# The first attention opens with the value rows of one token tile

## The chip, the core and the metric

The kernel runs on one core of a Trainium2 chip. TensorE (PE) multiplies, VectorE (DVE), ScalarE (ACT) and GpSimd (POOL) work on SBUF and PSUM, SyncE (SP) issues transfers; each of them works through its own queue of instructions in order and waits on semaphores. The metric is the time of one execution in device microseconds.

## The reference

Ten stages on a sequence of 256 tokens of width 1024, in float32. The first is a neighborhood attention; the others (a gated convolution, differential attention, a recurrent mixer and more) are not touched.

```
h   = rms_norm(x, g[0])
qkv = (h @ w_qkv).reshape(B, rows, 64, 3, 16 heads, 64)       # w_qkv: 1024 x 3072
s   = einsum(q / 8, k in a window of 8 x 16 neighbours) + bias
o   = softmax(s) @ v
m   = o @ w_o;  x = x + rms_norm(m, g[1])
```

## The kernel before

**Products.** A float32 matrix is split in two parts of type float32r, high and low (`w_hi`, `w_lo`; `hT_hi`, `hT_lo`), and a product is three matmuls: high x high, high x low, low x high. The tokens are two tiles of 128 (t = 0, 1). `hT` holds the normalised x turned, in 8 blocks of 128 rows, which are made in the order `BLOCKS = [0, 4, 1, 5, 2, 6, 3, 7]`.

**Slabs.** Weights come as slabs of 1 MB in the order of the list that `plan` makes. SP issues them into 3 buffers `raw` (a buffer is free when the slab three earlier is split: `lo_done`), ACT copies a slab into one of 5 buffers `w_hi` (`feed` in ACT's program, L719), DVE subtracts and writes `w_lo` (`feed` in DVE's program, L1298). Each engine calls `feed(n)` at places written out by hand; it works all slabs below n that are not done yet, and waits for each in turn. The first attention has 12 slabs: a column slab holds 256 columns of the query or key weights over all 1024 rows (in DRAM rows of 1 KB), a value slab 512 columns over 512 rows (rows of 2 KB). `COLUMN_SLABS` and `VALUE_SLABS` give their places: before, slabs 0 and 1 are query and key columns, 2 and 3 the first half of the values.

**Opening.** SP issues x's two tiles, slabs 0 to 2, six gain rows, 16 bias rows (`load_rpb`), four rows of taps, and then slab 3. ACT makes the squares of both tiles of x (L735), POOL the reciprocal roots (`powers`) and the high part of slab 0 (L610), DVE scales x (`normed`, L1337), PE turns it (`turn_x`, L2053), ACT and DVE split the turned blocks (`tile_parts`, L738 and L1320), tile 0 and then tile 1. `keep_busy(n)` puts n products of the identity, whose result nobody reads, into PE's queue.

**First attention.** Heads go in pairs (units). PE's order is `first_columns` (banks c0, c1 from slab 0, which starts with tile 1's first block ready), columns c2, c3 (keys, slab 1), scores of units 0 and 1 (`unit_scores`), the taps, then the value rows `value_rows(0, 0, kh, t)` of half 0 from slabs 2 and 3, with unit 0's turn of weights before the last of them. Columns are `half_columns` (24 matmuls of 256 columns of tokens a bank), value rows have 512 columns and one token tile. A result lies in one of 4 PSUM banks in the order of `BANK_ORDER` and is moved out by ACT: `columns_out`, `values_out`, `weights_turned` (L864, L924). Scores wait for the moved q and k. DVE adds the bias (`scores`), takes maxima, ACT the exponentials (`unit_exps`), DVE the quotient (`normalised`). Ahead of this DVE makes lambdas and rotary angles, ACT their sine and an exponential (L1255, L1257).

Of the kernel before, what the change touches and what calls it, by code (L numbers as in the profile page):

```python
# [20 lines left out]
ALU = mybir.AluOpType  # L21
ACT = mybir.ActivationFunctionType
# [18 lines left out]
RAW = 3  # L41
RING = 5
# [26 lines left out]
COLUMN_SLABS = {0: [0, 1, 4, 5, 8, 9, 10, 11], 3: [2, 3, 4, 5, 8, 9, 10, 11]}  # L69
VALUE_SLABS = {0: [2, 6], 3: [0, 6]}  # L70
BANK_ORDER = {0: "c0 c1 c2 c3 taps v0.0 v0.1 T0 c4 T1 c5 V0 V1 c6 c7 v1.0 v1.1 T2 T3 c8 c9 V2 V3 c10 c11 c12 c13"
# [201 lines left out]
def two_blocks(nc, w, out):  # L273
# [3 lines left out]
    with ctx:  # L277
# [82 lines left out]
        invf, ang, rot, turns = z(4096, 4128), z(4128, 4256, (2, T, 32)), z(4256, 4384), z(4384, 4512)  # L360
# [6 lines left out]

        landed = [sem(f"landed{i}") for i in range(RAW)]
        hi_done, lo_done = sem("hi_done"), sem("lo_done")
# [75 lines left out]
        def score_bank(u):  # L445
            return 2 * (u % 2)

# [88 lines left out]
        def _(sp):  # L536
            for t in range(T):
# [3 lines left out]
                    .then_inc(x_loaded[t], 16)  # L541
            for n, (src, k, c, _) in enumerate(slabs):
                if n == RAW:
                    early_rows(sp)
                    load_rpb(sp, 0, rpb_loaded)
                    tap_rows(sp)
# [16 lines left out]
        def _(pool):  # L563
# [43 lines left out]
            late_rows(pool)  # L607
            powers("pre0.1")
            pool.wait_ge(landed[0], 16)
            pool.tensor_copy(w_hi[:, 0, :], raw[:, 0, :]).then_inc(hi_done, 1)  # L610
# [3 lines left out]
            pool.wait_ge(hi_done, 2)  # L614
# [94 lines left out]
        def _(act):  # L709
            fed = [0]  # L710

            def feed(upto):
                while fed[0] < min(upto, n_slabs):
                    n = fed[0]
                    act.wait_ge(landed[n % RAW], 16 * (n // RAW + 1))
# [6 lines left out]
            def feed_half(i):  # L722
# [3 lines left out]
                act.wait_ge(landed[n % RAW], 16 * (n // RAW + 1))  # L726
# [201 lines left out]
            def attention0():  # L928
                b = B[0]
                columns_out(0, 2)  # L930
                columns_out(0, 3)
                feed(b + 4)
                unit_exps(0, 0)
                feed(b + 5)
                unit_exps(0, 1)
                weights_turned(0, 0)
                values_out(0, 0, 0)
                values_out(0, 0, 1)
                feed(b + 7)
                columns_out(0, 4)  # L940
                weights_turned(0, 1)
                feed(b + 8)
                columns_out(0, 5)
                turned_output(0)
                turned_output(1)
                feed(b + 9)
                columns_out(0, 6)
                columns_out(0, 7)
# [289 lines left out]
            for t in range(T):  # L1238
                pre(0, t)
# [1476 lines left out]
```

## Time and profile before

| | |
|---|---|
| median of 3 runs | 1209.8 us (1209.3 to 1210.08) |
| span of the profiled execution | 1208.0 us |
| PE busy | 1189.8 us, 98% |
| DVE, ACT, POOL busy | 939.8, 667.1, 150.4 us |
| mean granted clock of PE | 0.997 |

The span runs from the first to the last instruction of one profiled execution; the time of a run is the whole execution, and the profiled execution has no other time of its own than its span. Busy shares are means over ten stages: an engine that is idle off the chain that ends last costs nothing.

### The profile page before, as it was taken

The numbers are of one execution on the slowest core, as the hardware profiler recorded it, in microseconds if no ns is written. First come the engines' busy times: TensorE is split into PE (matmuls) and PEld (weight loads), VectorE is DVE, ScalarE is ACT, GpSimd is POOL, SyncE is SP. The second block draws the span as 40 slices with busy tenths as digits, with TensorE's granted clock in tenths as the row PEclk, the third lists the DMA queues.
The fourth block names the chain that finished last, engine by engine and source line by source line (L and its number), as shares of the span: only waits on it lengthen the run. The fifth ranks groups of instructions, "written<-read, shape, count | busy, mean of one in ns | idle before, by whom it ended". The sixth has DMA issues, their size and how long they took to land.

```text
span 1208.0 us, 17902 instructions
## 1 busy us (share of the span) xinstructions
PE 1189.8 (98%) x6979; PEld 1038.1 (86%) x6979; DVE 939.8 (78%) x1270; ACT 667.1 (55%) x1060; POOL 150.4 (12%) x275
## 2 busy tenths in 40 slices
PE   8999999999999999999999999999999999999997
PEld 7898888888889988888888988888897888888886
DVE  6767898888776679989887889777775968667765
ACT  5665654444767776544447755434676555444445
POOL 5300510000200012000002100000208420000002
PEclk9999999999999999999999999999999999999999
DMA  7847386555544445665555565655455146565540
GB/s 245 254 154 232 137 269 209 177 196 170 187 151 150 132 149 200 209 206 178 193 170 185 183 230 182 201 178 170 147 175 174 36 156 211 183 209 184 200 140 36
DMA packets 151640, 215.84 MB, mean 179 GB/s; under 512 B 6970, under 2 KB 116924, under 8 KB 151556
## 3 DMA queue, kind: packets, MB, share of 16 engines
q1 hardware_dynamic: 148092, 207.46, 52.2%
q0 software_dynamic: 1760, 3.94, 1.2%
q10 hardware_dynamic: 1704, 3.28, 0.8%
q8 instruction: 56, 0.92, 0.3%
q14 instruction: 28, 0.23, 0.1%
HBM read 213.60 MB, written 1.06 MB: 178 GB/s over the span
## 4 chain that ended last, share of the span: by engine, by line
PE 91%; DVE 4%; ACT 2%; issue 1%; POOL 1%; DMA 0%; POOLq 0%; ACTq 0%; DVEq 0%
PE work L2408 24%; PE work L2411 13%; PE acc L1996 10%; PE acc L1997 9%; PE acc L1998 9%; PE work L1996 5%; PE work L1998 5%; PE work L1997 5%; DVE w_lo L1298 1%; PE work L2397 1%; PE work L2385 1%; PE work L2399 1%; PE work L2018 1%; PE work L2526 1%; PE acc L2053 1%
## 5 line engine op out<-in xcount | busy, mean ns | idle before, releaser
L1298 DVE TENSOR_TENSOR w_lo<-raw,w_hi 128x2048 fp32r<-128x2048 f32 (+1 forms) x194 | 440.7, 2278 | 60.6 <-ACT w_hi L719 60.6
L719 ACT ACTIVATE w_hi<-raw 128x2048 fp32r<-128x2048 f32 (+2 forms) x193 | 365.2, 1898 | 69.5 <-PE work L2411 60.1
L2408 PE MATMUL work<-hT_both,w_hi 128*128 128x512 f32 x1280 | 318.8, 391 | 0.0
L2408 PEld LDWEIGHTS work<-hT_both,w_hi 128*128 128x128 f32 x1280 | 234.8, 188 | 45.2
L2411 PEld LDWEIGHTS work<-hT_both,w_lo 128*128 128x128 f32 x1280 | 174.6, 190 | 12.5
L2411 PE MATMUL work<-hT_both,w_lo 128*128 128x256 f32 x1280 | 178.5, 282 | 0.0
L1996 PE MATMUL acc<-w_hi,aux_hi 128*128 128x512 f32 x400 | 157.8, 395 | 0.0
L1997 PE MATMUL acc<-w_lo,aux_hi 128*128 128x512 f32 x400 | 156.7, 392 | 0.0
L1998 PE MATMUL acc<-w_hi,aux_lo 128*128 128x512 f32 x400 | 155.8, 390 | 0.0
L1085 ACT ACTIVATE aux_hi<-Z 128x256 fp32r<-128x256 f32 x88 | 36.9, 419 | 195.8 <-DVE Z L1722 107.8
L1693 DVE TENSOR_REDUCE Z<-work 128x256 f32<-128x512 f32 x88 | 60.6, 689 | 90.2 <-PE work L2411 88.5
L1998 PEld LDWEIGHTS acc<-w_hi,aux_lo 128*128 128x128 f32 x400 | 75.1, 188 | 16.5
L1996 PEld LDWEIGHTS acc<-w_hi,aux_hi 128*128 128x128 f32 x400 | 75.4, 189 | 13.7
L1997 PEld LDWEIGHTS acc<-w_lo,aux_hi 128*128 128x128 f32 x400 | 75.5, 189 | 12.2
L591 POOL TENSOR_SCALAR ms<-ssq 128x1 f32<-128x1 f32 x26 | 18.8, 724 | 529.6 <-ACT xn L735 444.6
L1996 PE MATMUL work<-hT_both,w_hi 128*128 128x256 f32 x272 | 78.2, 287 | 0.0
L1997 PE MATMUL work<-hT_both,w_hi 128*128 128x256 f32 x272 | 76.9, 283 | 0.0
L1998 PE MATMUL work<-hT_both,w_lo 128*128 128x256 f32 x272 | 76.9, 283 | 0.0
L864 ACT ACTIVATE Z<-work 128x512 f32<-128x512 f32 (+1 forms) x84 | 41.5, 509 | 52.0 <-PE work L1998 35.2
L1996 PE MATMUL acc<-w_hi,hT_both 128*128 128x512 f32 (+1 forms) x184 | 67.8, 368 | 0.6 <-DVE hT_both L1320 0.6
L1998 PE MATMUL acc<-w_hi,hT_both 128*128 128x512 f32 (+1 forms) x184 | 66.6, 362 | 0.0
L1997 PE MATMUL acc<-w_lo,hT_both 128*128 128x512 f32 (+1 forms) x184 | 66.5, 362 | 0.0
(271 smaller groups left out, 1782.4 us busy)
## 6 DMA issues: line engine op xcount, KB each, us to landing
raw<-in_ffn_w_in SPq DMA_DIRECT2D x44, 1024.0 KB, 5.2
raw<-in_ffn_w_out SPq DMA_DIRECT2D x22, 1024.0 KB, 5.0
raw<-in_w_gate SPq DMA_DIRECT2D x22, 1024.0 KB, 5.3
raw<-in_w_up SPq DMA_DIRECT2D x22, 1024.0 KB, 5.3
raw<-in_w_down SPq DMA_DIRECT2D x22, 1024.0 KB, 5.0
raw<-in_na_w_qkv SPq DMA_DIRECT2D x12, 1024.0 KB, 7.5
raw<-in_da_w_qkv SPq DMA_DIRECT2D x12, 1024.0 KB, 5.3
raw<-in_ple_w_gate SPq DMA_DIRECT2D x8, 1024.0 KB, 5.0
```

Of the source, the lines that this page charges most:

```text
L591: link(pool.tensor_scalar(ms[:, c + p:c + p + 1], ssq[:, c + p:c + p + 1], so_far, None, ALU.add))
L719: act.activation(w_hi[:, n % RING, 0:size], raw[:, n % RAW, 0:size], ACT.Copy).then_inc(hi_done, 1)
L864: act.activation(dst, src, func).then_inc(bank_free[g % WORK], 1)
L1085: act.activation(aux_hi[:, c % 2, :], hid32[:, c % 2, :], ACT.Copy).then_inc(hid_hi_done, 1)
L1298: dve.tensor_tensor(w_lo[:, n % RING, 0:size], raw[:, n % RAW, 0:size], w_hi[:, n % RING, 0:size].bitcast(F32), ALU.subtract).then_inc(lo_ ...
L1693: dve.tensor_reduce(src, bank(g).rearrange("p (e s) -> p s e", e=2), AX.X, ALU.add)\
L1996: pe.matmul(dst, stationary[0], moving[0], start=first, stop=False)
L1997: pe.matmul(dst, stationary[0], moving[1], start=False, stop=False)
L1998: return pe.matmul(dst, stationary[1], moving[0], start=False, stop=last)
L2018: ins = pe.transpose(b[0:width, i * P:i * P + rows], v, ident[0:rows, 0:rows])
L2408: pe.matmul(b.rearrange("p (e s) -> p e s", e=2), v[0][:, k, cols(c % 2)], hT_both[:, k, :, :], start=k == 0, stop=False)
L2411: ins = pe.matmul(b[:, 0:S], v[1][:, k, cols(c % 2)], hT_hi[:, k, :], start=False, stop=k == KT - 1)
```

## The change

Slabs 0 and 1 are now the first half of the values (`VALUE_SLABS` 0 and 6), and columns begin with slab 2. They come in four halves of 0.5 MB, each with two blocks of rows in the order of `BLOCKS`: half 0 between the tiles of x, half 1 behind tile 1, then 2 and 3. ACT makes the high part of halves 0 and 3, POOL of 1 and 2, DVE all four low parts, between its blocks of tile 0. PE begins with `first_rows` of tile 0 (it takes each block as it is split), turns x's tile 1 inside it, does tile 1's rows, then c0 to c3 and the rest. Two calls of `keep_busy` (8 and 2) go. ACT's four loads of lambda, positions, table and gains move behind tile 0's splits. ACT and DVE call `feed` and the evacuations in a new order. The angles lie in another place of `Z`.

```diff
+FIRST = 2
...
-COLUMN_SLABS = {0: [0, 1, 4, 5, 8, 9, 10, 11], 3: [2, 3, 4, 5, 8, 9, 10, 11]}
-VALUE_SLABS = {0: [2, 6], 3: [0, 6]}
-BANK_ORDER = {0: "c0 c1 c2 c3 taps v0.0 v0.1 T0 c4 T1 c5 V0 V1 c6 c7 v1.0 v1.1 T2 T3 c8 c9 V2 V3 c10 c11 c12 c13"
+COLUMN_SLABS = {0: [2, 3, 4, 5, 8, 9, 10, 11], 3: [2, 3, 4, 5, 8, 9, 10, 11]}
+VALUE_SLABS = {0: [0, 6], 3: [0, 6]}
+BANK_ORDER = {0: "v0.0 v0.1 c0 c1 c2 c3 taps c4 c5 T0 c6 T1 c7 V0 V1 v1.0 v1.1 T2 T3 c8 c9 V2 V3 c10 c11 c12 c13"
...
+        half_landed = [sem(f"half_landed{i}") for i in range(2 * FIRST)]
+        act_half_hi, pool_half_hi, half_lo = sem("act_half_hi"), sem("pool_half_hi"), sem("half_lo")
...
+        def landing(n):
+            return 16 * (n // RAW + (n % RAW >= FIRST))
+
+        def weight_half(v, i):
+            return v[:, i // 2, (i % 2) * (SLAB // 2):(i % 2 + 1) * (SLAB // 2)]
...
+            def value_half(i):
+                src = w["na_w_qkv"][0][:, 2 * D:2 * D + 512].rearrange("(b a p) n -> p a b n", b=2, p=P)
+                sp.dma_start(weight_half(raw, i).rearrange("p (b n) -> p b n", b=2), src[:, i, :, :])\
+                    .then_inc(half_landed[i], 16)
...
             for t in range(T):
                 src = w["x"][0]
                 sp.dma_start(x[:, t, :],
                              bass.AP(src.tensor, src.offset + 32 * t * D, [[D, 32], [64 * D, 4], [1, D]]))\
                     .then_inc(x_loaded[t], 16)
+                value_half(t)
+            value_half(2)
+            value_half(3)
             for n, (src, k, c, _) in enumerate(slabs):
+                if n < FIRST:
+                    continue
...
+            powers("pre0.0")
+            for i in (1, 2):
+                pool.wait_ge(half_landed[i], 16)
+                pool.tensor_copy(weight_half(w_hi, i), weight_half(raw, i)).then_inc(pool_half_hi, 1)
             powers("pre0.1")
-            pool.wait_ge(landed[0], 16)
-            pool.tensor_copy(w_hi[:, 0, :], raw[:, 0, :]).then_inc(hi_done, 1)
             for i in range(32):
                 ins = pool.memset(invf[:, i:i + 1], float(np.float32(10000.0) ** np.float32(-i / 32)))
             ins.then_inc(freq_ready, 1)
-            pool.wait_ge(hi_done, 2)
+            pool.wait_ge(hi_done, 1)
...
-                    act.wait_ge(landed[n % RAW], 16 * (n // RAW + 1))
+                    act.wait_ge(landed[n % RAW], landing(n))
...
+                feed(b + 6)
                 columns_out(0, 2)
+                feed(b + 7)
                 columns_out(0, 3)
-                feed(b + 4)
                 unit_exps(0, 0)
-                feed(b + 5)
                 unit_exps(0, 1)
+                feed(b + 8)
+                columns_out(0, 4)
+                columns_out(0, 5)
                 weights_turned(0, 0)
-                values_out(0, 0, 0)
-                values_out(0, 0, 1)
-                feed(b + 7)
-                columns_out(0, 4)
+                feed(b + 9)
+                columns_out(0, 6)
                 weights_turned(0, 1)
-                feed(b + 8)
-                columns_out(0, 5)
+                columns_out(0, 7)
                 turned_output(0)
                 turned_output(1)
...
-                feed(b + 9)
-                columns_out(0, 6)
-                columns_out(0, 7)
...
-            for t in range(T):
-                pre(0, t)
+            def high_half(i):
+                act.wait_ge(half_landed[i], 16)
+                act.activation(weight_half(w_hi, i), weight_half(raw, i), ACT.Copy).then_inc(act_half_hi, 1)
+
+            pre(0, 0)
+            high_half(0)
+            pre(0, 1, (0,))
+            evacuated(act, G["vec"])
+            tile_parts(0, 0, range(4))
+            pre(0, 1, (1,))
+            tile_parts(0, 0, range(4, 8))
+            high_half(3)
...
-            evacuated(act, G["vec"])
-            tile_parts(0, 0)
             tile_parts(0, 1)
-            act.wait_ge(hi_done, 1)
-            fed[0] = 1
+            fed[0] = FIRST
             feed(3)
+            values_out(0, 0, 0)
+            feed(4)
+            values_out(0, 0, 1)
             columns_out(0, 0)
+            feed(5)
             columns_out(0, 1)
...
-                    dve.wait_ge(hi_done, n + 1)
+                    dve.wait_ge(hi_done, n + 1 - FIRST)
...
-                feed(b + 3)
+                feed(b + 5)
                 expand(0)
+                expand(1)
+                feed(b + 6)
                 scores(0, 0)
-                expand(1)
+                scores(0, 1)
                 taps_out()
-                scores(0, 1)
-                feed(b + 4)
+                feed(b + 7)
                 normalised(0)
                 expand(2)
-                feed(b + 5)
                 normalised(1)
                 expand(3)
-                feed(b + 6)
-                feed(b + 7)
+                feed(b + 8)
                 turned_output(0)
                 turned_output(1)
-                feed(b + 8)
...
+            def low_half(i):
+                if i in (1, 2):
+                    dve.wait_ge(pool_half_hi, i)
+                else:
+                    dve.wait_ge(act_half_hi, 1 + i // 3)
+                dve.tensor_tensor(weight_half(w_lo, i), weight_half(raw, i), weight_half(w_hi, i).bitcast(F32),
+                                  ALU.subtract).then_inc(lo_done if i % 2 else half_lo, 1)
...
+            low_half(0)
+            tile_parts(0, 0, range(4))
+            low_half(1)
+            tile_parts(0, 0, range(4, 8))
             normed(0, 1)
-            tile_parts(0, 0)
+            low_half(2)
+            low_half(3)
             tile_parts(0, 1)
-            feed(2)
+            fed[0] = FIRST
+            feed(3)
             lambdas()
             rotary()
+            feed(4)
...
-            def first_columns():
...
+            def first_rows(t, kh):
+                g = G[f"v0.0.{t}"]
+                b = open_bank(pe, g) if kh == 0 else work[:, g % WORK, :]
+                for i in range(4):
+                    k, half = BLOCKS[4 * kh + i], 2 * kh + i // 2
+                    if t == 0 and i % 2 == 0:
+                        if half in (1, 2):
+                            pe.wait_ge(pool_half_hi, half)
+                        else:
+                            pe.wait_ge(act_half_hi, 1 + half // 3)
+                    split_done(pe, 0, t, k)
+                    for part in (hT_hi, hT_lo):
+                        pe.matmul(b, part[:, k, cols(t)], w_hi[:, kh, cols(i, 512)],
+                                  start=kh == 0 and i == 0 and part is hT_hi, stop=False)
+                if t == 0 and kh == 1:
+                    turn_x(0, 1)
+                for i in range(4):
+                    if t == 0 and i % 2 == 0:
+                        pe.wait_ge(lo_done if i else half_lo, kh + 1)
+                    ins = pe.matmul(b, hT_hi[:, BLOCKS[4 * kh + i], cols(t)], w_lo[:, kh, cols(i, 512)],
+                                    start=False, stop=kh == 1 and i == 3)
+                if kh == 1:
                     ins.then_inc(bank_full[g % WORK], 1)
+                elif t == 1:
+                    ins.then_inc(used, 1)
...
-                first_columns()
-                half_columns(0, 2)
-                half_columns(0, 3)
+                for t in range(T):
+                    first_rows(t, 0)
+                    first_rows(t, 1)
+                for n in range(4):
+                    half_columns(0, n)
                 unit_scores(0, 0)
                 unit_scores(0, 1)
                 turn_taps()
-                value_rows(0, 0, 0, 0)
-                value_rows(0, 0, 0, 1)
-                value_rows(0, 0, 1, 0)
+                half_columns(0, 4)
+                half_columns(0, 5)
                 unit_turn(0, 0)
-                value_rows(0, 0, 1, 1)
-                half_columns(0, 4)
+                half_columns(0, 6)
                 unit_turn(0, 1)
-                half_columns(0, 5)
+                half_columns(0, 7)
                 unit_values(0, 0)
                 unit_values(0, 1)
-                half_columns(0, 6)
-                half_columns(0, 7)
...
             turn_x(0, 0)
-            keep_busy(8)
             for ph, kind in enumerate(PHASES):
                 if kind in ("na", "da"):
                     if ph == 0:
-                        turn_x(0, 1)
-                        keep_busy(2)
```

## Rows read from the trace of the kernel before

**Rows 1.** The page: the span.

```profile
span 1208.0 us, 17902 instructions
```

**Rows 2.** PE's waits in the execution: us in total, times, longest.

```profile
PE work L2165 <- DVE hT_both L1320: 2.1, 1, 2.1
...
PE work L2018 <- DVE Z L1531: 1.0, 1, 1.0
```

**Rows 3.** PE in order of time, 14 to 43 us: start, us, engine, line.

```profile
14.96 5.87 PE L2165 MATMUL work<-hT_both,w_hi 128*128 128x256 f32 x32 [2.13 <-DVE hT_both L1320]
...
22.59 0.28 PE L1996 MATMUL work<-hT_both,w_hi 128*128 128x256 f32 x1
...
28.44 0.72 PE L2183 MATMUL acc<-Z 64*128 64x128 f32 x8
...
30.44 0.37 PE L2072 MATMUL work<-ident,Z 88*128 88x88 f32 x2
...
31.11 0.50 PE L1996 MATMUL work<-w_hi,hT_both 128*128 128x512 f32 x1
...
39.46 0.60 PE L2018 MATMUL work<-ident,Z 128*128 128x128 f32 x4
...
42.67 0.28 PE L1996 MATMUL work<-hT_both,w_hi 128*128 128x256 f32 x1
```

**Rows 4.** Busy time by engine in a stretch, granted clock, DMA share, GB/s.

```profile
16.00:19.30 3.30, 3.30 (x17) 3.27 (x16) 3.08 (x5) 3.14 (x6) 0.24 (x2) 0.50 0.79 233
```

**Rows 5.** SP's queue in order of time, 0 to 80 us.

```profile
9.57 13.55 SPq L528 DMA_DIRECT2D Z<-in_na_rpb  x16
...
24.91 37.95 SPq L553 DMA_DIRECT2D raw<-in_na_w_qkv  x9
```

**Rows 6.** Issues by line: ns shortest/median/longest, first and last start (L553: slabs 1 and 2).

```profile
L553 SPq DMA_DIRECT2D raw<-in_na_w_qkv x2: 582/1732/2881, 2.8 to 3.4; - x2
...
L508 SPq DMA_DIRECT2D Z<-in_norm_g x5: 279/296/1509, 6.3 to 8.9; - x5
...
L528 SPq DMA_DIRECT2D Z<-in_na_rpb x16: 677/766/1719, 9.6 to 22.3; - x16
L528 POOL DMA_DIRECT2D Z<-in_na_rpb x16: 563/602/774, 42.8 to 51.7; - x16
```

**Rows 7.** The page's DMA issues: KB each, us to landing (column slabs).

```profile
raw<-in_ffn_w_in SPq DMA_DIRECT2D x44, 1024.0 KB, 5.2
```

**Rows 8.** ACT, DVE and POOL in order of time, 6 to 17 us.

```profile
6.20 0.63 ACT L735 ACTIVATE xn<-x 128x512 f32<-128x512 f32 x1
...
7.35 0.88 DVE L1337 TENSOR_SCALAR xn<-x,rstd 128x512 f32<-128x512 f32 x2 [0.98 <-POOL rstd L596]
...
8.65 0.74 ACT L738 ACTIVATE hT_both<-acc,vecT 128x128 fp32r<-128x128 f32 x2 [1.12 <-PE acc L2053]
...
9.16 2.52 DVE L1337 TENSOR_SCALAR xn<-x,rstd 128x512 f32<-128x512 f32 x2 [0.92 <-POOL rstd L596]
...
9.40 2.00 POOL L610 CAST w_hi<-raw 128x2048 fp32r<-128x2048 f32 x1 [0.35 <-DMA raw<-in_na_w_qkv]
...
16.83 0.61 DVE L1320 SCALAR_TENSOR_TENSOR hT_both<-acc,vecT,hT_both 128x128 fp32r<-128x128 f32 x2 [0.18 <-ACT hT_both L738]
```

**Rows 9.** ACT and DVE in order of time, 16 to 42 us.

```profile
16.96 3.70 ACT L719 ACTIVATE w_hi<-raw 128x2048 fp32r<-128x2048 f32 x2
...
17.36 4.49 DVE L1298 TENSOR_TENSOR w_lo<-raw,w_hi 128x2048 fp32r<-128x2048 f32 x2
...
21.83 0.38 ACT L864 ACTIVATE Z<-work 128x256 f32<-128x256 f32 x1 [1.17 <-PE work L2170]
...
23.20 1.28 ACT L1255 ACT_TABLE_LOAD   x1
...
25.76 0.31 ACT L1255 ACTIVATE trig<-Z 128x128 f32<-128x128 f32 x1 [1.28 <-DVE Z L1948]
...
40.72 0.60 ACT L924 ACTIVATE Z<-work 64x512 f32<-64x512 f32 x1
```

More of the change, by code:

```diff
@@ L359, in two_blocks @@
         lamr, lamp = z(11864, 12120, (2, 2, 64)), z(12120, 12248, (2, 64))
-        invf, ang, rot, turns = z(4096, 4128), z(4128, 4256, (2, T, 32)), z(4256, 4384), z(4384, 4512)
+        invf, ang, rot, turns = z(3584, 3616), z(3616, 3744, (2, T, 32)), z(3744, 3872), z(3872, 4000)
         ebr = z(9216, 9728, None, 8)
@@ L725, in feed_half @@
                 half = slice(i * size, (i + 1) * size)
-                act.wait_ge(landed[n % RAW], 16 * (n // RAW + 1))
+                act.wait_ge(landed[n % RAW], landing(n))
                 if n >= RING:
@@ L1304, in feed_half @@
                 half = slices(slabs[n][1] * slabs[n][2] // 2)[i]
-                dve.wait_ge(hi_done, n + 1)
+                dve.wait_ge(hi_done, n + 1 - FIRST)
                 ins = dve.tensor_tensor(w_lo[:, n % RING, half], raw[:, n % RAW, half],
@@ L2154, in half_columns @@
                 ins.then_inc(bank_full[g % WORK], 1)
-            def first_columns():
-                v = w_hi[:, 0, :].rearrange("p (k n) -> p k n", k=KT)
-                pe.wait_ge(hi_done, 1)
-                for c in range(2):
-                    b = open_bank(pe, G[f"c0.{c}"])
-                    for k in BLOCKS:
-                        if c == 0:
-                            split_done(pe, 0, 1, k)
-                        for part in (hT_hi, hT_lo):
-                            pe.matmul(b[:, 0:S], v[:, k, cols(c)], part[:, k, :], start=k == 0 and part is hT_hi, stop=False)
-                v = slab(0)[1]
-                for c in range(2):
-                    g = G[f"c0.{c}"]
-                    for k in range(KT):
-                        ins = pe.matmul(work[:, g % WORK, 0:S], v[:, k, cols(c)], hT_hi[:, k, :],
-                                        start=False, stop=k == KT - 1)
+            def first_rows(t, kh):
[20 more added lines that the diff above has]
+                if kh == 1:
                     ins.then_inc(bank_full[g % WORK], 1)
+                elif t == 1:
+                    ins.then_inc(used, 1)
             def unit_scores(ph, u):
@@ L2376, in first_tile @@
                     for i in range(2):
-                        pe.wait_ge(hi_done, b0 + i + 1)
+                        pe.wait_ge(hi_done, b0 + i + 1 - FIRST)
                     for k in ks:
```

## The prediction

> **What bounds the kernel now.** I read the page first (the span), then who waited for whom on TensorE, then the instructions in order of time in the first 60 us, then SyncE's queue. The span is 1208.0 us [rows 1] and the median of the runs 1209.8, so 1.8 us lie around the span; the sum below is made within the span and carried over to 1209.8. TensorE's longest wait in the whole execution is the one ahead of its first product (2.1 us), and the one hole that it meets later in the first attention is 1.0 us, before a turn of softmax weights [rows 2]. So the kernel is a row of products, and what the opening can win or lose is the time at which that row gets past the first attention's first columns. The reader is to see five points on TensorE [rows 3]: the first product at 14.96, columns c0 and c1 done at 22.59, c2 and c3 at 28.44, scores and taps done at 31.11, the first half of the values done at 42.67. The 48 value products took 11.56 less the 0.35 of the turn that lies among them (39.46 to 39.81): 11.2 us, 0.233 each. Columns c2 and c3 took 5.85 for 48, or 0.122 each, 2.9 a bank. Scores take 1.0 a unit, the taps 0.67.
>
> In the changed order the same work, c0 to c3, both value tiles, two scores and the taps, ends with the taps. Before had all of it at 42.67 - 0.35 = **42.3**. What the change brings is the time at which the new order gets there, less 42.3, because from there on the two orders hold the same products.
>
> **The opening.** The work on x's tile 0 stays: its squares end at 6.20, DVE scales it at 7.35, ACT's first split of a turned block starts at 8.65 [rows 8]. The first half slab takes the queue place of x's tile 1, which was there by 6.20. ACT copies half a slab in 0.95 (half of 1.85), DVE makes a low half in 1.1 (half of 2.25) [rows 9], so the low half runs from 8.25 to 9.35 behind the scaling, the first low block is ready at 9.7, and TensorE starts there: **5.2 us earlier** than 14.96. It doesn't run through. On DVE now lie, one behind the other: four low blocks to 10.9 (0.79 for two [rows 8]), the second low half to 12.0, four blocks to 13.5, tile 1's scaling (0.88) to 14.4, two low halves to 16.7, and tile 1's eight blocks to 19.8. Tile 0's products end inside that, at about 17; tile 1's follow without a hole, 24 x 0.233 = 5.6, to 22.7. The third slab (c0, c1) is copied by ACT after tile 1's splits, from 19.6 to 21.4, and by DVE to 23.7; c0 and c1 then end at 23.7 + 5.8 = 29.5.
>
> The two casts on POOL are the weak place. Now a scaling pair that takes 0.88 alone took 2.52 where POOL's cast of a slab (9.40, 2.00) lay over it [rows 8]. So a cast beside a DVE instruction can cost from 0 up to its own length, 1.0 for a half, twice: c1 ends between 29.5 and 31.5. I take 30.5. The Trainium skill (SBUF — State Buffer, "SBUF: two separate sides") says that a VectorE instruction with two SBUF inputs and a GpSimd instruction that reads SBUF exclude each other for the whole instruction. That speaks against giving POOL two casts beside DVE's low halves; the 2.52 agrees with such an exclusion, and by that rule c1 would end at 31.5.
>
> If nothing else were late, TensorE would now be 3.4 us ahead: at 30.5 it lacks c2, c3, scores and taps, 5.8 + 2.67 = 8.4, and before stands 8.4 ahead of its 42.3 at 33.9; 33.9 - 30.5 = 3.4.
>
> **What is late next: the fourth slab.** Columns c2 and c3 need the slab of key columns, number 3. Before used slab 3 only for the second half of the value rows' sum, at 31.11 + 24 x 0.233 = 36.7. It is the first that SyncE issues behind the bias rows and taps, and it was issued at 24.91, though its buffer was free earlier [rows 5]. The change leaves that order, and puts two more issues ahead of it. How early can it go? In before three issues were held up: the third slab's (2.88 against 0.58), the first gain row's (1.51 against 0.30) and one of the bias rows' (1.72 against 0.68) [rows 6]: 2.3 + 1.2 + 1.0 = 4.5 us. Two more issues cost 1.2. From below, with no hold-up left: 24.9 - 4.5 + 1.2 = 21.6. From above, with all of it kept: 26.1. The halves have rows of 2 KB where slabs 0 and 1 had 1 KB, so fewer packets stand ahead, and the two extra issues pass while the queue drains; I keep one hold-up of the smaller kind, 1.1: **22.7**. The Trainium skill (Perfetto Trace Analysis, "DMA Instruction — HWDGE (DVE, Sync)") has the profiled time of an issue hold the wait for the descriptor generator and the generation, which runs into a full buffer. By that page fewer rows ahead mean shorter issues, which would move the sum to the lower bound; no row of before shows which of the three was which.
>
> From 22.7: a column slab lands 5.2 us after its issue where the queue is empty [rows 7]: 27.9. ACT's copy 1.85: 29.8. DVE's low part 2.3: **32.1**. So c2 starts at 32.1, not at 30.5, and the 1.0 to 2.0 of the casts and any slow clock in the opening are covered by this wait: the cover is 1.6 us on my value, and what goes over it is paid one for one. c3 ends at 37.9.
>
> **And the fifth: ACT's order.** ACT is the engine behind the scores, and its queue is in order. From 29.8 it has: tile 1's value rows, two activations of 0.60 [rows 9], to 31.0; c0, 0.3, 31.3; slab 4, landed 3.2 after slab 3 (the spacing of 6.20 and 9.40 [rows 8]) at 31.1, copied to 33.2; c1 33.5; the sine with its table load, 1.28 + 0.31, 35.1; the exponential's table load 36.4; then feed(b + 6), slab 5, 38.3; and only then c2, 38.7. c2 had been ready in PSUM since 35.0. unit_scores(0, 0) needs it, so it runs from 38.7 to 39.7; feed(b + 7) holds c3 until 40.9; unit_scores(0, 1) from 40.9 to 41.9; taps to **42.6**. Slabs 4 to 6 land in time for this: slab 5's buffer is free at 23.7, slab 6's at 32.1, and it has until 38.7. The table loads and slab copies hid behind products before; here they lie on the path, 1.7 us of it (a path of c3's end at 37.9, 0.35 for its evacuation, 2.67 for scores and taps would give 40.9).
>
> **The sum.** 42.6 - 42.3 = **+0.3 us**: of the 5.2 us won at the first product DVE's queue leaves 3.4; slab 3 takes 1.6 of it, c3's evacuation 0.35, ACT's order 1.7. As a line: end = issue of slab 3 + 19.9. From the bounds 21.6 and 26.1: 41.5 to 46.0, or -0.8 to +3.7.
>
> Behind it I price the rest at nothing. The first turn of weights needs the softmax of unit 0: DVE makes slab 4, two expansions, slab 5, two scores, the taps and slab 6 first and reaches the weights at about 47.4; TensorE has c4 and c5 until 42.6 + 5.8 = 48.4. That cover is 1.0 us; without it the turn would wait the difference. The hole at 108 hangs on the last two units' scores and softmax [rows 2], which move with TensorE, so it neither gives nor takes. The moved ACT issues (lambda, positions, table, gains: four) fall at about 15, where ACT waits for tile 1's turn; the removed ten filler products were no one's input, but they kept TensorE busy: see the clock.
>
> **Rivals.** (1) **The gain is kept**: slab 3 isn't late. It decides from an issue at about 20.0 on. That wants the bias rows to go out at POOL's pitch (0.60 each [rows 6]) instead of SyncE's 13.55 for 16 [rows 5]: 13.55 - 9.6 = 4.0 earlier than 22.7, so 18.7, low part at 28.1. Then the path is c1 at 30.5, c2 and c3, evacuation, scores and taps: 39.4, -2.9: **1206.9**. For it: before held issues up while much traffic stood ahead. Against it: the shortest bias row was 0.68 on SyncE, held up or not. (2) **The queue is held as before**, the slower side: slab 3 goes out at or after 24.9. It decides from there: 24.9 + 19.9 = 44.8, +2.5, **1212.3**, and at 26.1 **1213.5**. For it: the bytes ahead of the fourth slab are the same, and the issue comes two places later. Against it: the biggest hold-up belonged to a third whole slab, and there are fewer rows. (3) **The clock**: in before the granted clock was 0.50 (1.2 of 2.4 GHz) from 16.0 to 19.3 [rows 4], after the stretch in which TensorE waited 2.1 us, and the 32 products there took 5.87 instead of 32 x 0.122 = 3.9: 2.0 lost. The new opening has shorter but more waits and no fillers. A low stretch before c1's end is covered by slab 3; one on c4 to c7, after the waits of the scores, is paid in full: +0.3 + 2.0, **1212.1**; with a somewhat later slab 3 it passes the bound. That the change alters nothing that can be told is the likeliest case itself.
>
> **How the numbers follow.** A measurement of this kernel tells about 0.2% (2.4 us) from no change. The likeliest case, slab 3 issued between 21.6 and 24.8, has 0.52: -0.8 to +2.4, 1209.0 to 1212.2, at 1210.1. Rival 1 has 0.18; rival 2 0.2; rival 3 0.1, half of it within the bound beside an early slab 3. Faster by over 0.2%: 0.2 (rival 1, and 0.02 for a shorter ACT path in the likeliest). Slower by over 0.2%: 0.27 (rival 2, half of rival 3, 0.02 for casts that go over their cover). Within: the remaining 0.53. The range reaches to rival 1's time and near the upper bound of slab 3: 1206.9 to 1213.2.
>
> **What would show it.** Right: TensorE's first product near 9.7; a wait of TensorE's columns for DVE's low part of 1 to 3 us that ends near 32; SyncE's slab 3 near 22.7; waits of the score products for ACT's evacuations near 38 and 41 that follow slab copies; the taps near 42.6; the rest of the trace shifted by the same amount. Wrong: no wait for slab 3 (rival 1), its issue after 24.9 (rival 2), a clock of 0.50 behind the scores (rival 3), or a wait of the first turn of weights for DVE, which I priced at nothing.

## The result

The changed kernel takes 1212.1 us (median of 9 runs, 1210.8 to 1213.4) against 1209.3 for the kernel before beside it (9 runs): a ratio of 1.0027, 95% interval 1.0019 to 1.0035. It is **slower by 2.8 us**, inside the prediction's range. The 0.2% that the prediction takes as no change lies just inside the interval. The likeliest case ended at +2.4 and at 1212.2: the difference is just outside it, the time just inside, because the kernel before measured 1209.3 here and 1209.8 ahead of the prediction. The times of the kernel before lie in two groups some 2 us apart (of the 15 beside experiments 8 to 10, seven from 1207.5 to 1208.2 and eight from 1209.3 to 1210.4), so its median depends on the mix, and its profiled execution (span 1208.0) is of the upper group. The profiled execution of the changed kernel took 1212.35 with a span of 1210.6 and a mean granted clock of 0.996.

Who TensorE waited for in the changed kernel (us in total, times, longest; line 2038 is the column products, 1327 DVE's low part of a slab):

```profile
PE work L2038 <- DVE w_lo L1327: 4.7, 2, 4.2
...
PE work L2060 <- DVE Z L1560: 1.0, 1, 1.0
PE work L2210 <- DVE hT_both L1349: 0.9, 1, 0.9
```

In [rows 2] no slab was waited for; now one costs 4.2 us. In order of time on TensorE, to be held against [rows 3]:

```profile
9.95 2.06 PE L2210 MATMUL work<-w_hi,hT_both 128*128 128x512 f32 x8 [0.91 <-DVE hT_both L1349]
...
24.78 0.39 PE L2038 MATMUL work<-hT_both,w_hi 128*128 128x256 f32 x1 [0.44 <-DVE w_lo L1327]
...
35.03 0.58 PE L2038 MATMUL work<-hT_both,w_hi 128*128 128x256 f32 x1 [4.23 <-DVE w_lo L1327]
...
39.66 0.28 PE L2038 MATMUL work<-hT_both,w_hi 128*128 128x256 f32 x1
...
42.98 0.71 PE L2233 MATMUL acc<-Z 64*128 64x128 f32 x8
43.98 0.72 PE L2233 MATMUL acc<-Z 64*128 64x128 f32 x8
...
45.64 0.38 PE L2038 MATMUL work<-hT_both,w_hi 128*128 128x256 f32 x1
```

The first product comes 5.0 us earlier (14.96 to 9.95). c1 is done at 24.78 + 5.85 = 30.6, where before had the same amount of work done at 33.9: 3.3 ahead. Then TensorE stands until 35.03 (4.23 us of it is the wait for slab 3's low part). Scores and taps are done at 45.64, where before stood at 42.3: +3.3. Later points that both kernels share are late by 2.8 (scores of units 2 and 3 from 59.23, before from 56.40; the ffn's first product at 143.4, before at 140.6; the last product of that line at 1165.0, before at 1162.4, which is 2.6), so next to nothing is won back behind the opening.

SyncE's queue of the changed kernel, against [rows 5]; and the gain rows' issues (ns shortest/median/longest), against [rows 6]:

```profile
4.47 0.53 SPq L572 DMA_DIRECT2D raw<-in_na_w_qkv  x1
5.04 4.93 SPq L517 DMA_DIRECT2D Z<-in_norm_g  x5
...
10.36 12.79 SPq L537 DMA_DIRECT2D Z<-in_na_rpb  x16
...
24.93 31.40 SPq L572 DMA_DIRECT2D raw<-in_na_w_qkv  x8
```

```profile
L517 SPq DMA_DIRECT2D Z<-in_norm_g x5: 295/296/3455, 5.0 to 9.7; - x5
```

Slab 3 goes out at 24.93, before at 24.91. It lands at 30.74, where ACT had waited for it 7.11 us. Behind it come the copies of slabs 4 (34.03), 5 (39.26) and 6 (41.33), with the evacuations of c2 (41.06) and c3 (43.13) among them (ACT, in order of time):

```profile
30.74 1.91 ACT L740 ACTIVATE w_hi<-raw 128x2048 fp32r<-128x2048 f32 x1 [7.11 <-DMA raw<-in_na_w_qkv]
...
34.03 1.91 ACT L740 ACTIVATE w_hi<-raw 128x2048 fp32r<-128x2048 f32 x1
...
39.26 1.90 ACT L740 ACTIVATE w_hi<-raw 128x2048 fp32r<-128x2048 f32 x1
41.06 0.36 ACT L885 ACTIVATE Z<-work 128x256 f32<-128x256 f32 x1
41.33 1.90 ACT L740 ACTIVATE w_hi<-raw 128x2048 fp32r<-128x2048 f32 x1
43.13 0.37 ACT L885 ACTIVATE Z<-work 128x256 f32<-128x256 f32 x1
```

And the stretches behind the wait (columns as in [rows 4]: busy time and count of PE, PEld, DVE, ACT, POOL, then granted clock):

```profile
33.00:36.00 3.00, 0.97 (x4) 0.97 (x5) 2.00 (x2) 2.99 (x5) 0.00 (x0) 0.50 0.89 280
36.00:39.00 3.00, 3.00 (x16) 3.00 (x15) 3.00 (x3) 2.95 (x4) 0.00 (x0) 0.50 0.90 286
39.00:42.00 3.00, 3.00 (x25) 3.00 (x24) 2.26 (x4) 2.99 (x5) 0.00 (x0) 0.90 0.97 307
```

The granted clock is 0.50 (1.2 of 2.4 GHz) where the wait ends. The first 21 column products behind it took 39.66 - 35.03 = 4.63 us; at the 0.122 each of the later ones they are 2.56, so 2.1 are lost.

### The profile page after: what moved, and what is told of

It reads as the page before. It is cut to its first block, busy times and chain, and to the rows that moved or that the text cites. A ratio compares the mean times of both kernels' runs of the same rounds, so it can differ in the third digit from the quotient of the medians.

```text
span 1210.6 us, 17870 instructions
## 1 busy us (share of the span) xinstructions
PE 1188.5 (98%) x6959; PEld 1035.8 (86%) x6959; DVE 939.3 (78%) x1272; ACT 667.4 (55%) x1061; POOL 147.9 (12%) x276
## 4 chain that ended last, share of the span: by engine, by line
PE 90%; DVE 4%; ACT 2%; SPq 2%; issue 1%; DMA 0%; POOL 0%; POOLq 0%; ACTq 0%; DVEq 0%
PE work L2456 24%; PE work L2459 13%; PE acc L2038 10%; PE acc L2039 9%; PE acc L2040 9%; PE work L2038 5%; PE work L2039 5%; PE work L2040 5%; DVE w_lo L1327 2%; PE work L2445 1%; PE work L2433 1%; PE work L2447 1%; PE work L2060 1%; PE work L2574 1%; SPq L537 1%
## 5 line engine op out<-in xcount | busy, mean ns | idle before, releaser
L1327 DVE TENSOR_TENSOR w_lo<-raw,w_hi 128x2048 fp32r<-128x2048 f32 (+1 forms) x192 | 436.0, 2276 | 64.4 <-ACT w_hi L740 64.4
L740 ACT ACTIVATE w_hi<-raw 128x2048 fp32r<-128x2048 f32 (+1 forms) x192 | 363.5, 1898 | 73.0 <-PE work L2459 59.7
L2459 PE MATMUL work<-hT_both,w_lo 128*128 128x256 f32 x1280 | 178.5, 282 | 0.0
L2038 PE MATMUL work<-hT_both,w_hi 128*128 128x256 f32 x288 | 83.9, 291 | 4.7 <-DVE w_lo L1327 4.7
L2039 PE MATMUL work<-hT_both,w_hi 128*128 128x256 f32 x288 | 82.3, 286 | 0.0
L2040 PE MATMUL work<-hT_both,w_lo 128*128 128x256 f32 x288 | 82.2, 286 | 0.0
```

Source lines behind the costliest of these rows:

```text
L740: act.activation(w_hi[:, n % RING, 0:size], raw[:, n % RAW, 0:size], ACT.Copy).then_inc(hi_done, 1)
L1327: dve.tensor_tensor(w_lo[:, n % RING, 0:size], raw[:, n % RAW, 0:size], w_hi[:, n % RING, 0:size].bitcast(F32), ALU.subtract).then_inc(lo_ ...
L2038: pe.matmul(dst, stationary[0], moving[0], start=first, stop=False)
L2039: pe.matmul(dst, stationary[0], moving[1], start=False, stop=False)
L2040: return pe.matmul(dst, stationary[1], moving[0], start=False, stop=last)
L2459: ins = pe.matmul(b[:, 0:S], v[1][:, k, cols(c % 2)], hT_hi[:, k, :], start=False, stop=k == KT - 1)
```

## The experiments

**The theory** after the result: slab 3's place behind the bias rows makes TensorE wait 4.2 us; the low clock comes of the wait; and ACT's order (two slab copies and two table loads ahead of c2 and c3) is a second gate of the scores just behind. **The rivals**: ACT's order alone is the loss; the clock alone is; the hold-up belongs to the gain rows and not to the place in the queue.

Times are medians; the ratio is to the kernel before, run beside each. A trace shows one execution. Fillers are products of the identity whose result nobody reads.

**1. Slab 3 first, nothing else** (slab3_first).

```diff
-                if n == RAW:
+                if n == RAW + 1:
                     early_rows(sp)
                     load_rpb(sp, 0, rpb_loaded)
                     tap_rows(sp)
```

> SyncE issues slab 3 ahead of the gain rows, bias rows and taps; slab 4 comes behind them. Theory S (the late slab 3 is the loss, nothing else): slab 3 goes out near 12.2 us, TensorE's 4.2 us wait ahead of c2 is gone, the taps end at 30.5 + 5.8 + 0.4 + 2.7 = 39.4 instead of 45.6, and the time is 1212.1 - 6.2 = 1205.9. Theory A (ACT's in-order queue is a second gate behind it): slab 4 now lands near 32.5, ACT waits for it with c1's, c2's and c3's evacuations behind, so scores of unit 0 start near 40, of unit 1 near 42.4, taps end near 44.1: 1210.6. Theory C (the low clock on c2 is the loss): the wait and with it the low clock go, 2.2 us: 1209.9.

1217.2 us, ratio 1.0068 (1.0056 to 1.0080): the worst of all. The wait for slab 3 goes (c2 starts at 31.62), but slab 4 is now the one behind the bias rows. ACT meets its copy ahead of c1's, c2's and c3's evacuation. ACT, TensorE and a stretch of this kernel:

```profile
35.88 1.91 ACT L740 ACTIVATE w_hi<-raw 128x2048 fp32r<-128x2048 f32 x1 [7.13 <-DMA raw<-in_na_w_qkv]
...
42.91 0.36 ACT L885 ACTIVATE Z<-work 128x256 f32<-128x256 f32 x1
```

```profile
43.42 1.23 PE L2233 MATMUL acc<-Z 64*128 64x128 f32 x8 [5.78 <-ACT Z L885]
```

```profile
45.00:48.00 3.00, 2.73 (x26) 1.69 (x20) 2.30 (x4) 1.61 (x9) 0.00 (x0) 0.50 0.47 133
```

The wait moved on, grew to 5.78 us, and the low clock came with it (8 score products take 1.23 us instead of 0.71). SyncE's first gain row goes out at 12.84 here, 8 us behind slab 2 and right behind slab 3, and no gain row takes more than 0.52 us: the long issue on the first of them is gone (one bias row takes 1.79).

**2. Bias rows on POOL's queue** (bias_pool).

```diff
-                    load_rpb(sp, 0, rpb_loaded)
...
             ins.then_inc(freq_ready, 1)
+            load_rpb(pool, 0, rpb_loaded)
```

> The 16 bias rows go out on POOL's queue behind its memsets of the frequencies, so slabs 3, 4 and 5 follow their free buffers (about 12, 18, 25 us). Theory S: taps end at 39.4, 1205.9. Theory A: with slab 4 early ACT is held less, scores of unit 0 start near 36.5, unit 1 near 38.4, taps end at 40.1: 1206.6. Theory C: 1209.9. Against all of them: if POOL's 16 issues delay the masks that the bias needs past 38 us, the scores are late on DVE and the first turn of weights waits.

1213.9, ratio 1.0037 (1.0025 to 1.0049). SyncE is free for slab 3 at 12.12. But POOL issues the bias rows from 15.2 to 24.8, and the slab that SyncE issues in that time (18.23) and the one right behind it (24.86) land late:

```profile
L571 SPq DMA_DIRECT2D raw<-in_na_w_qkv x2: 368/378/389, 18.2 to 24.9; - x2
...
DMA to landing us min/median/max: 10.3/12.2/14.1
```

Slab 4 lands 14.1 us after its issue (slab 3 of the changed kernel 5.8), ACT holds c2 behind it, the scores wait 2.97, and the clock is 0.50 to 0.66 from 42 to 51. Taps come 1.3 earlier than in the changed kernel (43.70 against 44.97), the first turn of weights 1.4 later (52.87 against 51.49).

**3. ACT's order alone** (act_order): evacuations ahead of slab copies.

```diff
             values_out(0, 0, 0)
-            feed(4)
             values_out(0, 0, 1)
             columns_out(0, 0)
-            feed(5)
-            columns_out(0, 1)
             act.wait_ge(rot_ready, 1)
...
+            columns_out(0, 1)
+            feed(4)
...
                 feed(b + 6)
                 columns_out(0, 2)
-                feed(b + 7)
                 columns_out(0, 3)
+                feed(b + 7)
```

> ACT moves the value rows, c0 and c1 out and makes the sine and exponential before slab 3 lands, and moves c2 and c3 out before it copies slab 6. Theory A as the prediction had it (ACT's order costs 1.7 us by itself): 1210.4. Theory S, with the clock as it was seen: c3 ends at 43.0 on TensorE anyway, ACT has c2 out at 41.4 and c3 at 43.5, so no more than 0.2 to gain: 1211.9 to 1212.1.

1213.6, ratio 1.0039 (1.0027 to 1.0051): no gain. ACT and TensorE:

```profile
31.72 3.70 ACT L740 ACTIVATE w_hi<-raw 128x2048 fp32r<-128x2048 f32 x2
```

```profile
36.00 0.58 PE L2037 MATMUL work<-hT_both,w_hi 128*128 128x256 f32 x1 [5.13 <-DVE w_lo L1326]
```

TensorE now waits 5.13 us for slab 3, the clock behind it is 0.50, and the scores start at 43.53. The new order has a cost of its own: slab 3 landed at 30.5 (issue at 24.68, 5.8 to landing), but its copy starts at 31.72, behind two table loads and c1's evacuation, so 1.2 us of the wait are ACT's. The run shows that this order gains nothing; it doesn't show what ACT's order costs by itself.

**4. Fillers in the wait** (fill: nine between c1 and c2; fill16: sixteen).

```diff
                 for n in range(4):
+                    if n == 2:
+                        for _ in range(9):
+                            pe.matmul(acc[:, 3, 0:P], ident[:, :], ident[:, :], start=True, stop=True)
                     half_columns(0, n)
```

> Nine products of the identity between c1 and c2 (about 3.9 us of the 4.2 us wait); their result is not read. Theory C (the low clock on c2 is the loss): c2 takes 2.9 us instead of 5.1 and all of it is gained, 1209.9. Theory A: c3 ends near 40.8, but unit 0's scores wait for ACT's c2 at 41.4 and unit 1's for c3 at 43.5, taps at 45.2: 1211.7. Theory S: the wait for slab 3 stays 4.2 us with the fillers in it.

1213.6, ratio 1.0042 (1.0029 to 1.0054). Nine fillers took only 2.2 us (31.0 to 33.1), 2.64 of the wait were left, and the clock was 0.56 from 36 to 39, so this run says nothing on a full clock; the next has sixteen.

> As fill, with 16 products of the identity, 3.9 us, which fill the wait for slab 3 nearly to its end (9 of them had taken 2.2 us and left 2.6 us open, and the clock fell all the same). Theory C: c2 and c3 run at the full clock, 2.2 us less than after's time. Theory A: unit 0's scores then wait for ACT's c2 near 41.4, unit 1's for c3 near 43.5, taps at 45.2 against 45.6: 0.4 us less, and a low clock may come behind those waits instead.

1212.5, ratio 1.0033 (1.0021 to 1.0046). Now the clock is full on c2 and c3 (1.00 from 33 to 45), and what lay behind it shows on TensorE, with a stretch behind the taps:

```profile
35.46 0.39 PE L2038 MATMUL work<-hT_both,w_hi 128*128 128x256 f32 x1 [0.66 <-DVE w_lo L1327]
...
42.01 0.71 PE L2233 MATMUL acc<-Z 64*128 64x128 f32 x8 [0.53 <-ACT Z L885]
44.08 0.71 PE L2233 MATMUL acc<-Z 64*128 64x128 f32 x8 [1.01 <-ACT Z L885]
45.08 0.37 PE L2114 MATMUL work<-ident,Z 88*128 88x88 f32 x2
```

```profile
45.00:48.00 3.00, 3.00 (x23) 2.72 (x16) 2.90 (x10) 2.72 (x15) 0.00 (x0) 0.64 0.95 316
```

The taps start at 45.08, in the changed kernel at 44.97. The 2.1 us of low clock are made up, and a later slab 3 (0.4) and the waits for ACT (1.5) take nearly all of it: the second gate stands at nearly the same point as the first. Behind the waits of 0.53 and 1.01 the clock falls after all, to 0.64 and then 0.79 from 45 to 51, and the first turn of weights comes at 53.09 (changed kernel 51.49). This execution was the slowest of the five (1214.2), so the median may not pay that.

**5. Fillers and ACT's order** (act_fill16): sixteen fillers with experiment 3's order, changed in one place: slab 3's copy (`feed(4)`) and c1's evacuation lie ahead of the exponential, which takes away experiment 3's own delay. The edit is shown against 3.

```diff
+            feed(4)
+            columns_out(0, 1)
             act.wait_ge(lam_sum, 1)
...
-            columns_out(0, 1)
-            feed(4)
...
+                        for _ in range(16):
+                            pe.matmul(acc[:, 3, 0:P], ident[:, :], ident[:, :], start=True, stop=True)
```

> Sixteen fillers, and ACT's order with the exponential's table load behind slab 3's copy and c2 and c3 moved out before slab 6 is copied. If clock and ACT's order hide one another (each alone brings 0 to 0.4 us), both together bring c3's end at 40.8, scores from 41.0, taps at 43.9 against 45.6: 1.8 us less than after, 1 us over before (ratio 1.0009). If only slab 3's lateness counts, no less than after (ratio 1.0027).

1210.5, ratio 1.0017 (1.0008 to 1.0025). Scores at 40.67 and 41.67 without a wait, taps at 42.67. Sixteen fillers alone and experiment 3's order alone gave nothing; fillers and this order bring 1.2 us against the changed kernel by the ratios (1.0027 to 1.0017), with intervals that overlap. What this order brings without fillers was not run.

**6. Fillers in the kernel before** (before_fill): keep_busy(9) in the place of keep_busy(2).

```diff
                         turn_x(0, 1)
-                        keep_busy(2)
+                        keep_busy(9)
```

> The kernel before with seven more products of the identity in TensorE's 2.1 us wait ahead of its first product. Theory C (the low clock follows a wait and costs 2.0 us there): the 32 products take 3.9 us instead of 5.9, time less 2.0 (ratio 0.9983). Rival: the first 16 products are paced by the blocks that DVE splits (0.39 each, the last at 17.4), so full clock brings only 20.7 - 19.6 = 1.1 us (ratio 0.9991). If the clock stays low in spite of the fillers: no change.

1209.0, ratio 1.0001 (0.9992 to 1.0010). In the profiled execution the low stretch of [rows 4] is gone (1.00 from 13 to 19.3, scores at 26.21 instead of 28.44), but the median doesn't move. And most of those 2.2 us aren't the fillers'. DVE, POOL and TensorE:

```profile
9.03 0.88 DVE L1337 TENSOR_SCALAR xn<-x,rstd 128x512 f32<-128x512 f32 x2 [0.92 <-POOL rstd L596]
```

```profile
10.06 1.89 POOL L610 CAST w_hi<-raw 128x2048 fp32r<-128x2048 f32 x1 [1.15 <-DMA raw<-in_na_w_qkv]
```

```profile
13.29 4.85 PE L2165 MATMUL work<-hT_both,w_hi 128*128 128x256 f32 x32
```

In this execution slab 0 landed at 10.06, behind DVE's scaling of tile 1, which took 0.88. In the one of [rows 8] it landed at 9.40, POOL's cast lay over the scaling, and that took 2.52. This is 1.6 us, and the first product came 1.67 earlier here. To the clock at most 1.0 is left: the 32 products take 4.69 (13.29 to 17.98) at 1.00 and took 5.71 (14.96 to 20.67) with the low clock in them. This kernel has two groups of times as well, five from 1207.4 to 1207.8 and six from 1209.0 to 1211.1, and this execution (1207.38) is the lowest of the eleven. That the cast's place makes the two groups fits these two traces, but is not shown.

**7. Slab 3 first and both orders** (reordered): experiment 1, and ACT and DVE work slabs 4 to 7 in other places, so that fewer evacuations and steps of the softmax are queued behind a slab that hasn't landed. ACT's and then DVE's part are shown.

```diff
-                if n == RAW:
+                if n == RAW + 1:
...
-            feed(3)
+            feed(4)
             values_out(0, 0, 0)
-            feed(4)
             values_out(0, 0, 1)
             columns_out(0, 0)
-            feed(5)
             columns_out(0, 1)
...
-                feed(b + 6)
                 columns_out(0, 2)
-                feed(b + 7)
+                feed(b + 5)
                 columns_out(0, 3)
+                feed(b + 6)
                 unit_exps(0, 0)
                 unit_exps(0, 1)
+                feed(b + 7)
...
-            feed(3)
+            feed(4)
             lambdas()
             rotary()
-            feed(4)
...
-                feed(b + 5)
                 expand(0)
                 expand(1)
-                feed(b + 6)
+                feed(b + 5)
                 scores(0, 0)
                 scores(0, 1)
                 taps_out()
-                feed(b + 7)
                 normalised(0)
-                expand(2)
+                feed(b + 6)
                 normalised(1)
+                expand(2)
+                feed(b + 7)
                 expand(3)
```

> Slab 3 is issued ahead of the bias rows, DVE makes its low part right behind slab 2's, ACT moves c2 out before it copies slab 4 and c3 right behind, and DVE makes the bias before slab 4's low part and the weights before slab 5's. Theory S+A (slab 3's place on SyncE and ACT's order together hold the opening's gain back, each alone moves the wait): no wait of TensorE over 1 us up to the taps, no low clock, c2 near 31, c3 done near 36.8, taps done near 40.0 against before's 42.3; with 0.6 lost at slab 5 the time is before less 1.5 to 2.0 us (ratio 0.9984 to 0.9988). Rival M (the queue's bytes are the limit, so the wait moves on again): slab 4, now behind the bias rows, lands near 36, its low part is ready at 40 or later, c4 waits 1 to 3 us and the clock falls behind that wait: before or slower.

1208.1, ratio 0.9997 (0.9988 to 1.0006). No big wait on TensorE and no low clock in the opening:

```profile
36.73 0.72 PE L2231 MATMUL acc<-Z 64*128 64x128 f32 x8
37.73 0.71 PE L2231 MATMUL acc<-Z 64*128 64x128 f32 x8
38.73 0.37 PE L2112 MATMUL work<-ident,Z 88*128 88x88 f32 x2
```

Some 4 us are back against the changed kernel (1.0027 to 0.9997 is 3.6). The 1.5 to 2.0 below the kernel before that were expected aren't there: from before it can't be told. The trace has the taps done at 39.5, earlier than expected, but the 42.3 that they were held against is of an execution of before's upper group; in experiment 6's execution the same point comes at 40.3 (c4 from 40.63, less the 0.35 of the turn).

**8. The two orders without slab 3** (orders_only): experiment 7 with slab 3 in the changed kernel's place.

```diff
-                if n == RAW + 1:
+                if n == RAW:
```

> The reordered kernel's orders of ACT and DVE, but slab 3 back in its place behind the bias rows and taps. Theory (slab 3's issue sets the end, the orders only take away what is queued behind it): issue at 24.9, c2 near 35.0 with a wait of 4 us or more on TensorE, low clock behind it, scores near 42 to 43, taps near 45: 1211 to 1212, 0 to 1 below the changed kernel. Rival (ACT's order was the loss all along): scores near 39 to 40, 1209 or less.

1213.5, ratio 1.0038 (1.0024 to 1.0052). The slab-3 move alone stands at 1.0068, the orders alone at 1.0038, both at 0.9997: neither gains by itself. Expected was 0 to 1 us below the changed kernel, measured 1 above, with overlapping intervals. These orders are made for an early slab 3: ACT copies it ahead of the value rows, so the first value row is moved out at 31.04 (changed kernel 22.43), and with slab 3 late they have a cost of their own. The profiled execution was the fastest of the five (1211.4), and its trace doesn't show what the median pays: slab 3 goes out at 23.89, TensorE waits 2.79 for it, and the clock stays full.

```profile
33.40 0.39 PE L2036 MATMUL work<-hT_both,w_hi 128*128 128x256 f32 x1 [2.79 <-DVE w_lo L1326]
```

**9. Gain rows behind the bias rows** (rows_later).

```diff
-                    early_rows(sp)
                     load_rpb(sp, 0, rpb_loaded)
                     tap_rows(sp)
+                    early_rows(sp)
```

> The changed kernel with the six gain rows issued behind the bias rows and taps instead of ahead of them. Theory (the hold-up belongs to the place in the queue, not to the kind of transfer): the first bias row is held 2 us or more, the gain rows take 0.3 each, slab 3 goes out at 24.5 to 25.5 as before. Rival (the hold-up belongs to the gain rows' own descriptors): the first bias row takes 0.7, slab 3 goes out at about 22 if the gain rows then pass unheld, and TensorE's wait for it shrinks by 2.5.

A single run, 1212.75. SyncE's queue, and the bias rows' issues:

```profile
5.38 15.38 SPq L537 DMA_DIRECT2D Z<-in_na_rpb  x16
...
22.55 1.65 SPq L517 DMA_DIRECT2D Z<-in_norm_g  x5
...
24.58 30.73 SPq L572 DMA_DIRECT2D raw<-in_na_w_qkv  x8
```

```profile
L537 SPq DMA_DIRECT2D Z<-in_na_rpb x16: 677/730/2994, 5.4 to 20.0; - x16
```

The long issue is now the first bias row's, the gain rows take 0.3 each, and slab 3 goes out at nearly the same time (24.58): the hold-up belongs to the place behind the slabs.

**10. Slab 8 behind the second turn** (reordered2): experiment 7 with one more place of ACT changed.

```diff
-                feed(b + 9)
                 columns_out(0, 6)
                 weights_turned(0, 1)
+                feed(b + 9)
                 columns_out(0, 7)
```

> The reordered kernel with one place changed: ACT moves c6 and the second turn of weights out before it waits for slab 8. In the reordered kernel that wait (2.43 us for the slab's landing at 51.17) lay ahead of the turn's evacuation, and TensorE's product of values waited 0.75 us for it. Theory (what is left is ACT's queue in order): that wait goes, the time falls by 0.7 to about 1207.4, 1.4 below before. Rival (the two orders end alike, because scores of units 2 and 3 then wait for c7's evacuation, which now lies behind the copy): the wait shows up at c7, and the time stays at 1208.1.

1207.3, ratio 0.9987 (0.9979 to 0.9996): **faster than before**, by 1.6 us, and than the changed kernel by 4.8 (1.0027 to 0.9987). The wait of the value products for ACT (0.75 in 7) is gone. That this one place brought the gain is not shown: the intervals of 7 and 10 overlap, and the profiled execution (1208.5) is one of the two slowest of eleven, with a wait for ACT and a low clock that the median need not have:

```profile
38.44 0.72 PE L2231 MATMUL acc<-Z 64*128 64x128 f32 x8 [0.71 <-ACT Z L885]
```

```profile
42.00:45.00 3.00, 3.00 (x20) 3.00 (x20) 2.86 (x11) 3.00 (x17) 0.00 (x0) 0.68 0.91 328
```

Nine of the eleven times lie from 1206.6 to 1207.6 (middle 1207.2), and before's lower group from 1207.5 to 1208.2 (middle 1207.7): over that group the gain is some 0.5 us, and most of the 1.6 is that eight of before's fifteen times are of the upper one.

## Why the prediction was in range and on the wrong side

- **First product**: 9.7 predicted, 9.95 measured. Right. The 14.96 and 42.3 that the sum starts from are of one execution of before, with POOL's cast over the scaling; experiment 6's execution has them at 13.29 and 40.3, so against such an execution the change could win 2.0 us less.
- **DVE's queue and the casts**: c1's end 30.5 (29.5 to 31.5), measured 30.6. The two casts on POOL took 1.04 and 1.90 us; the second began 0.2 behind the start of DVE's second low half. The Trainium skill (SBUF — State Buffer, "SBUF: two separate sides") has such a pair exclude each other for the whole instruction; 1.90 is 1.04 with most of that low half's 1.22 in it, so this trace agrees, with POOL as the one that waited. Only one of the two casts was stretched, and c1's end came nearer to 30.5 than to 31.5. The cost lay under the wait for slab 3, as priced.
- **Issue of slab 3: the step that failed.** 22.7 was taken from 21.6 to 26.1, with one hold-up of 1.1 left of 4.5. Measured 24.93. The gain row was held 3.46 - 0.30 = 3.2 and one bias row about 0.4: 3.6 of hold-up instead of 1.1. It is no accident of one execution: in the six traces with SyncE's order of the changed kernel slab 3 goes out at 23.9 to 26.2, never as early as 22.7, and the first gain row takes 2.7 to 4.0. The argument that fewer packets and two more issues would let the queue drain was wrong: the third slab's hold-up went over to the first small transfer, and experiment 9 moved it once more with hardly a change for slab 3. So rival 2, a chance of 0.2, is what happened: 1212.3 for an issue at 24.9, measured 1212.1.
- **Landing**: 5.2 taken, 5.81 measured: 0.6 more (5.2 to 5.8 in the other traces with that order).
- **Low part and c2**: 4.2 from landing to c2 predicted, 4.3 measured (30.74 to 35.03). Right. c2 starts at 35.03 instead of 32.1.
- **The gate of the scores**: predicted was ACT (c2 and c3 out behind slab copies and table loads), with a full clock on c2 and c3. Measured was TensorE itself at 0.50, 2.1 us lost there. Rival 3 had a low clock behind the scores; it came one step earlier, behind the wait for slab 3. Its price of 2.0, from 32 products at 0.122, is too high for the stretch that it was read from: without the low clock these products took 4.69 and not 3.9 (experiment 6), so 1.0 was lost there. Experiment 4 shows ACT's gate just under it: by either, the taps start near 45.0. That "issue of slab 3 + 19.9" holds though its last steps were others is luck, as two gates of nearly the same length stood in one place: 24.93 + 19.9 + 0.6 = 45.4, measured 45.64.
- **The first turn of weights**, priced at nothing: it comes at 51.49, right behind c4 and c5 and without a wait. Right.
- **The sum**: +0.3 predicted at the taps, +3.3 measured there and +2.8 at the end; 2.8 of the 3.0 between them are slab 3's issue (2.2) and landing (0.6). Experiments 1, 7 and 8 show that the issue is the cause only together with the orders of ACT and DVE: with the orders kept, an earlier slab 3 makes it worse, and only both changes together give the loss back. How much of it is the clock's and how much ACT's is not shown, as the two hide one another (experiments 4 and 5).
- **Bias rows at POOL's pitch (rival 1)**: on SyncE they kept their pitch, 0.68 to 1.13 us each; on POOL's own queue they went at 0.60 (9.64 for 16), but the slabs beside them landed late (10.3 and 14.1 us).

What stays open: why the first small transfer behind the slabs is held, what decides in which executions the clock falls (experiments 4, 8 and 10), and what makes the two groups of times of the kernel before.

## What to carry to other kernels

An opening that starts earlier brings forward the due time of every slab behind it: look up the first slab whose issue stands behind small transfers, and follow it through copy, low part and evacuation before counting the gain. Where several in-order queues meet at one product, test the repairs together as well as singly: here the slab's move alone cost 5 us more and the orders alone gained nothing, and the pair gave back 4. A hold-up in an issuing queue isn't taken away by changing what is held: here it fell on whatever came first behind the opening's slabs at 5 us, and it was gone only where the small transfers began 8 us later. And look at the spread of the kernel that you compare with: when its times lie in two groups, a single trace of it is one of them.

## What the runs showed of the hardware

- The long issue behind the slabs moves with the place: 3.46 us on the first gain row, 2.99 on the first bias row when that came first. Slab 2, where the 2.88 of [rows 6] lay before, now took 0.53. With the first gain row 8 us later (12.6 to 12.8, experiments 1, 7 and 10) no gain row took more than 0.53.
- A slab of 1 MB that SyncE issued while POOL issued sixteen bias rows in 9.64 us landed after 14.1 us, the one right behind them after 10.3.
- Waits of TensorE and the granted clock behind them: 0.50 behind waits of 2.97, 3.79, 4.23, 5.13 and 5.78 us, 0.56 behind one of 2.64 with fillers ahead of it, full behind one of 2.79 (experiment 8). Waits of no more than 1.01 were followed by 0.64 and 0.79 (experiment 4) and by 0.75 and 0.68 (experiment 10). So the length of a wait alone doesn't tell the clock behind it in these traces.
- DVE's scaling of tile 1 took 2.52 us with POOL's cast over it and 0.88 where the cast began behind it (experiment 6); in the changed kernel POOL's second cast, begun beside a low half on DVE, took 1.90 instead of 1.04.
